# The indexer's scores from split, stacked operands instead of fp32

## The reference

```
iq = i_q.reshape(bsz, seq, IDX_HEADS, IDX_DIM)          # 16 heads of 64
ik = layernorm(i_k, idx_k_ln_g[l], idx_k_ln_b[l])       # one key of 64 for all heads
iw = i_w * (IDX_HEADS ** -0.5) * (IDX_DIM ** -0.5)
...
rel = jax.nn.relu(jnp.einsum('bthd,bsd->bths', iqb, ik))
score = jnp.einsum('bths,bth->bts', rel, iwb)
score = jnp.where(causal[None], score, -jnp.inf)
_, idx = lax.top_k(score, topk)                         # topk = 128
```

## Time and profile before

| | |
|---|---|
| median of 3 runs | 2920.77 us |
| lowest, highest | 2913.46, 2920.83 us |
| profiled execution | 2919.38 us |
| its span, first to last instruction | 2918.1 us |
| mean granted TensorE clock | 0.974 of full speed |
| busy share: TensorE, VectorE, ScalarE, GpSimd | 95%, 38%, 36%, 44% |
| chain that ended last: share of TensorE | 78% |
| the eight query projections and their scores | 1295 to 1437 us of the span |

### The profile page before, as it was taken

The page is one execution under the profiler, slowest core; times in us unless marked ns, Lnnn a source line. Parts: engine busy times, 40 slices in busy tenths (PEclk is TensorE's granted clock), DMA queues, the critical chain, the costliest instruction groups (busy, mean ns, idle before and its releaser), DMA issues.

```text
span 2918.1 us, 31494 instructions
## 1 busy us (share of the span) xinstructions
PE 2772.0 (95%) x12512; PEld 2208.8 (76%) x12512; DVE 1095.5 (38%) x1696; ACT 1045.7 (36%) x1727; POOL 1272.9 (44%) x638
## 2 busy tenths in 40 slices
PE   7579999999999999999999999999999999999999
PEld 5557788887777778866787777776777787788787
DVE  7967744442121131142376343334232213212200
ACT  5123333333333342232343444344343333433311
POOL 5664333433433354442334433343444444554743
PEclk9679999999999999999999999999999999999999
DMA  9745322222222214421222222222223322333343
GB/s 348 260 171 199 137 73 73 80 73 76 83 87 81 89 69 148 144 90 65 73 77 79 94 91 86 92 100 70 94 104 102 109 99 99 105 117 116 120 151 105
DMA packets 102961, 323.27 MB, mean 111 GB/s; under 512 B 11424, under 2 KB 14496, under 8 KB 102304
## 3 DMA queue, kind: packets, MB, share of 16 engines
q1 hardware_dynamic: 99072, 307.64, 30.8%
q10 hardware_dynamic: 3744, 13.63, 1.3%
HBM read 304.45 MB, written 16.78 MB: 110 GB/s over the span
## 4 chain that ended last, share of the span: by engine, by line
PE 78%; DVE 10%; POOL 4%; ACT 3%; DMA 2%; issue 2%; SPq 0%; DVEq 0%; ACTq 0%
PE bank L582 23%; PE bank L584 22%; PE bank L583 22%; POOL wlo L1652 2%; PE bank L824 2%; DVE TA L1295 2%; PE bank L812 2%; PE bank L743 2%; PE bank L845 1%; DVE TA L1475 1%; POOL Hlo L1673 1%; PE bank L804 1%; DMA TA<-in_strip 1%; PE bank L671 1%; DVE Y L1295 1%
## 5 line engine op out<-in xcount | busy, mean ns | idle before, releaser
L1652 POOL TENSOR_TENSOR wlo<-wraw,whi 128x1024 fp32r<-128x1024 f32 (+2 forms) x454 | 1054.9, 2325 | 1483.4 <-ACT whi L883 1483.4
L582 PE MATMUL bank<-Hhi,whi 128*128 128x512 f32 x3024 | 1245.8, 412 | 25.2 <-POOL Hlo L1673 16.7
L583 PE MATMUL bank<-Hlo,whi 128*128 128x512 f32 (+1 forms) x3152 | 1229.3, 390 | 0.0
L584 PE MATMUL bank<-Hhi,wlo 128*128 128x512 f32 x3024 | 1190.2, 394 | 0.0
L582 PEld LDWEIGHTS bank<-Hhi,whi 128*128 128x128 f32 x3024 | 574.8, 190 | 189.4 <-issue 48.8
L883 ACT ACTIVATE whi<-wraw 128x1024 fp32r<-128x1024 f32 (+2 forms) x454 | 456.8, 1007 | 702.2 <-PE bank L584 701.2
L583 PEld LDWEIGHTS bank<-Hlo,whi 128*128 128x128 f32 x3152 | 604.2, 192 | 126.1 <-issue 13.5
L584 PEld LDWEIGHTS bank<-Hhi,wlo 128*128 128x128 f32 x3024 | 573.6, 190 | 124.6
L1295 DVE SCALAR_TENSOR_TENSOR TA<-TA,par 128x1024 f32<-128x1024 f32 x60 | 128.0, 2133 | 9.1 <-DMA TA<-in_w_ada 3.4
L1248 DVE TENSOR_TENSOR TA<-bank,rows 128x512 f32<-128x512 f32 x48 | 33.0, 688 | 235.3 <-PE bank L584 235.3
L945 ACT ACTIVATE TA<-bank 128x512 f32<-128x512 f32 x64 | 38.0, 594 | 205.4 <-PE bank L584 205.4
(11 more groups left out here) (225 smaller groups left out, 2632.1 us busy)
## 6 DMA issues: line engine op xcount, KB each, us to landing
wraw<-in_w_in SPq DMA_DIRECT2D x304, 512.0 KB, 3.2
TA<-in_w_ada SPq DMA_DIRECT2D x64, 512.0 KB, 4.9
Y<-in_w_ada SPq DMA_DIRECT2D x32, 512.0 KB, 4.0
wraw<-in_w_out SPq DMA_DIRECT2D x32, 512.0 KB, 3.2
wraw<-in_w_o SPq DMA_DIRECT2D x32, 512.0 KB, 3.2
wraw<-in_w_mem ACTq DMA_DIRECT2D x16, 512.0 KB, 5.6
tmp_mgs<-TA SPq DMA_DIRECT2D x32, 256.0 KB, 2.0
TA<-tmp_mgs SPq DMA_DIRECT2D x32, 256.0 KB, 3.6
```

Source lines behind the costliest of these rows:

```text
L582: e.matmul(out, hi[:, c], xhi[k], start=first and j == 0, stop=False)
L583: e.matmul(out, hi[:, c], xlo[k], start=False, stop=False)
L584: m = e.matmul(out, lo[:, c], xhi[k], start=False, stop=last and end)
L1652: e.tensor_tensor(M.wlo[b][:, 0:w], M.wraw[b][:, 0:w], M.whi[b][:, 0:w].bitcast(F32), ALU.subtract).then_inc(S.lo)
```

## The change

Query and key are split for the scores as the large operands are. For the key, the 64 features lie twice on the 128 partitions; the rounded part goes to `ikp[0]` on all 128 and the remainder to `ikp[1]`. For each head, a buffer holds the rounded query on its own 64 partitions and its remainder on the other 64. One product on 128 rows of this stack with `ikp[0]` gives the sum of rounded x rounded and remainder x rounded; a second, on 64 rows, adds rounded x remainder of the key. The buffers are in Ohi and Olo.

The rounded parts are made by ScalarE and the remainders by VectorE, in a new post step for iq (first slot of the following projection, before the score step there) and at the end of the key's post step. The other engines get an empty step of the same place.

```diff
+        ohi, olo = self.pair["o"]
+        self.iqs, self.ikp = ((ohi[0], ohi[1]), (ohi[2], ohi[3])), (olo[0], olo[1])
...
     def index(j):
-        mark = moved("iq")
-
         def run():
-            Q, K = M.W2["Q"][j % 2], M.W2["K"][0]
-            pe.wait_ge(S.ik, 1)
-            pe.wait_ge(*mark)
+            K = M.ikp
+            pe.wait_ge(S.ikr, 1)
+            pe.wait_ge(S.iqr, 2 * j + 2)
             for hh in range(2):
-                r = slice(64 * hh, 64 * hh + 64)
+                r, Q = slice(64 * hh, 64 * hh + 64), M.iqs[j % 2][hh]
                 for i in (3, 2, 1):
-                    w = P * (i + 1)
+                    c, w = slice(i * P, (i + 1) * P), P * (i + 1)
                     bank = (BS0, BS1)[i % 2]
                     pe.wait_ge(*free[bank])
-                    e.matmul(M.banks[bank][:, 0:w], Q[r, i * P:(i + 1) * P], K[r, 0:w], start=True,
-                             stop=True).then_inc(S.ix)
+                    e.matmul(M.banks[bank][:, 0:w], Q[:, c], K[0][:, 0:w], start=True, stop=False)
+                    e.matmul(M.banks[bank][:, 0:w], Q[r, c], K[1][r, 0:w], start=False, stop=True).then_inc(S.ix)
...
# ScalarE, at the end of the key's post step
+        act.wait_ge(S.ik, 1)
+        e.activation(M.ikp[0], M.dst("ik"), ACT.Copy).then_inc(S.ikh)
+
+    def iq(j):
+        mark = moved("iq")
+
+        def run():
+            act.wait_ge(*mark)
+            act.wait_ge(S.ix, 6 * (j - 1))
+            for hh in range(2):
+                r = slice(64 * hh, 64 * hh + 64)
+                e.activation(M.iqs[j % 2][hh][r, :], M.dst("iq", j)[r, :], ACT.Copy).then_inc(S.iqh)
+            yield from rest(0)
+        return run()
...
# VectorE, at the end of the key's post step
+        dve.wait_ge(S.ik, 1)
+        dve.wait_ge(S.ikh, 1)
+        e.tensor_tensor(M.ikp[1], b, M.ikp[0].bitcast(F32), ALU.subtract).then_inc(S.ikr)
+
+    def iq(j):
+        mark = (S.evd, n["evd"])
+
+        def run():
+            dve.wait_ge(*mark)
+            for hh in range(2):
+                r, o = slice(64 * hh, 64 * hh + 64), slice(64 - 64 * hh, 128 - 64 * hh)
+                Q = M.iqs[j % 2][hh]
+                dve.wait_ge(S.iqh, 2 * j + hh + 1)
+                e.tensor_tensor(Q[o, :], M.dst("iq", j)[r, :], Q[r, :].bitcast(F32), ALU.subtract).then_inc(S.iqr)
+            yield from rest(0)
+        return run()
...
# TensorE's, ScalarE's and VectorE's posts get iq, GpSimd's and SyncE's get iq=idle(0)
```

More of the change, by code:

```diff
@@ L346, in __init__ @@
         self.ikq, self.ikl, self.ik = sem("ikq"), sem("ikl"), sem("ik")
+        self.ikh, self.ikr, self.iqh, self.iqr = sem("ikh"), sem("ikr"), sem("iqh"), sem("iqr")
         self.ix, self.ir, self.ia, self.top = sem("ix"), sem("ir"), sem("ia"), sem("top")
@@ L864, in tensor_program @@
             mem_k=mem_k, mem_v=mem_v, decay=silu, hq=silu, hv=turn("hv"), hz=silu, aq=norm("aq", ones),
-            ak=norm("ak", ones), av=turn("av"), az=silu, ik=ik, cq=norm("cq", ones), cg=silu, ckv=ckv,
+            ak=norm("ak", ones), av=turn("av"), az=silu, ik=ik, iq=lambda j: rest(0), cq=norm("cq", ones), cg=silu, ckv=ckv,
             bk=norm("bk", ones64), bv=turn("bv"), gate=silu, bq=norm("bq", ones64), bg=silu, qa=norm("qa", ones),
@@ L1169, in scalar_program @@
             mem_k=mem_k, mem_v=mem_v, decay=decay, hq=silu("hq"), hv=lambda h: rest(0), hz=silu("hz"),
-            aq=norm("aq"), ak=norm("ak"), av=lambda h: rest(0), az=silu("az"), ik=ik, cq=norm("cq"), cg=silu("cg"),
+            aq=norm("aq"), ak=norm("ak"), av=lambda h: rest(0), az=silu("az"), ik=ik, iq=iq, cq=norm("cq"), cg=silu("cg"),
             ckv=ckv, bk=norm("bk"), bv=lambda: rest(0), gate=gate, bq=norm("bq"), bg=silu("bg"), qa=norm("qa"),
@@ L1639, in vector_program @@
             mem_k=lambda h: rest(1), mem_v=lambda h: rest(1), decay=decay, hq=silu("hq"), hv=turn("hv"),
-            hz=silu("hz"), aq=norm("aq"), ak=norm("ak"), av=turn("av"), az=silu("az"), ik=ik, cq=norm("cq"),
+            hz=silu("hz"), aq=norm("aq"), ak=norm("ak"), av=turn("av"), az=silu("az"), ik=ik, iq=iq, cq=norm("cq"),
             cg=silu("cg"), ckv=ckv, bk=norm("bk"), bv=turn("bv"), gate=gate, bq=norm("bq"), bg=silu("bg"),
@@ L1761, in gpsimd_program @@
             mem_k=mem_k, mem_v=mem_v, decay=decay, hq=silu("hq"), hv=idle(0), hz=silu("hz"), aq=idle(1), ak=idle(1),
-            av=idle(0), az=silu("az"), ik=idle(1), cq=idle(1), cg=silu("cg"), ckv=ckv, bk=idle(1), bv=idle(0),
+            av=idle(0), az=silu("az"), ik=idle(1), iq=idle(0), cq=idle(1), cg=silu("cg"), ckv=ckv, bk=idle(1), bv=idle(0),
             gate=gate, bq=idle(1), bg=silu("bg"), qa=idle(1), ka=idle(1), va=idle(0), ga=silu("ga"))))
@@ L1883, in sync_program @@
             mem_k=idle(1), mem_v=idle(1), decay=idle(2), hq=idle(2), hv=idle(0), hz=idle(2), aq=idle(1), ak=idle(1),
-            av=idle(0), az=idle(2), ik=idle(1), cq=idle(1), cg=idle(2), ckv=lambda i: rest(2 * i), bk=idle(1),
+            av=idle(0), az=idle(2), ik=idle(1), iq=idle(0), cq=idle(1), cg=idle(2), ckv=lambda i: rest(2 * i), bk=idle(1),
             bv=idle(0), gate=idle(2), bq=idle(1), bg=idle(2), qa=idle(1), ka=idle(1), va=idle(0), ga=idle(2))))
```

## The result

The changed kernel takes 2949.02 us in the median of four runs (2937.33 to 2950.66), before 2920.8; the ratio is 1.0091 with a 95% interval of 1.0069 to 1.0113. It is slower: the medians lie 28.2 us apart, the ratio stands for 26.6 us. It took 30.6 us more than the profiled execution of before; 4.2 of these lie ahead of the changed stretch, whose start varies between 1283.5 and 1294.4 us over the profiled executions of this study.

The account below looks back on a forecast made before the run. TensorE, busy 95% of the span, was taken to bound the kernel. Products -7.9, wait +18.8 and clock +8.0 gave +18.9 us, so 2940 us, with a range of 2920 to 2948.

Parts of the forecast that it names:

- cheaper products: Score steps: two fp32r products replace each fp32 one, gaining 0.31 us per long and 0.19 per short step, 7.9 in all.
- TensorE's wait: Before each tile's first score product TensorE waits for VectorE's subtractions: 2.35 us per tile, 18.8 for eight.
- lower clock: Behind 5.6 of 8 TensorE waits a 3.4 us stretch at 1.2 GHz, 1.43 us each: 8.0 us, bounds 0 and 11.4.
- The price of the change of rows: Score steps: alternating 128-row and 64-row fp32r products cost as in fp32, 0.38 us; steps take 2.045 and 1.09 us.
- rival B: Score steps: changing rows costs fp32r products nothing, gain 26.9 us; 2914 us, up to 2925 with low clock; chance 0.13.
- The chain of the wait: From a tile's last projection product (P) through ScalarE, GpSimd and VectorE: TensorE ready at P + 3.59, goes on at P + 5.83.
- Rival C: VectorE's 64-partition subtractions are not held by GpSimd: wait 7.2 us in all, clock stays, 2920 us; chance 0.07.
- rival E: Score stage costlier: more than one low-clock stretch after a wait, or 64-row fp32r products dearer than fp32; 2945 to 2960; chance 0.08.
- Rival D: TensorE's wait before the scores is as forecast, but the clock stays up: 2932 us; chance 0.20.

Follow-up runs that it names:

- 128-row runs: Changed kernel with both score products on 128 rows: steps in place 2929.09 us, one slot later 2897.07, one slot later with zeros made earlier 2890.91.
- e3_gpsimd_after: Changed kernel, but GpSimd's weight remainder behind each query tile waits until VectorE's two subtractions are done: 2921.89 us, ratio 1.0011.
- e1_fill9: Changed kernel with nine extra 512-column products per query tile in front of TensorE's wait for the subtractions: 2929.11 us, ratio 1.0037.
- e9_fill6: Changed kernel with six extra products per query tile in front of TensorE's wait: 2935.75 us, ratio 1.0052.
- e2_fill3: Changed kernel with three extra products per query tile in front of TensorE's wait: 2938.29 us, ratio 1.0064.
- after: The changed kernel itself, with nothing further edited, against the kernel before: 2949.02 us, ratio 1.0091.
- e6_128_rows: Changed kernel with both products of each score on 128 rows (key's remainder padded with zeros), score steps in their place: 2929.09 us, ratio 1.0037.

## Why the prediction was right

The direction came out, and so did the three causes: cheaper products, the wait, the clock behind it. The first two terms were right to 1.3 us and the third was too small by 7, so the sum fell short by 8 us of 27.

| term of the sum | forecast | measured | from |
|---|---|---|---|
| cheaper products | -7.9 | -8.2 | 148.1 - 156.3 |
| TensorE's wait | +18.8 | +20.1 | 168.2 - 148.1 |
| lower clock | +8.0 (0 to 11.4) | +15.0 | 183.2 - 168.2 |
| sum | +18.9 | +26.9 | 183.2 - 156.3 |

**The price of the change of rows** held to hundredths: short step 1326.64 - 1325.56 = 1.08 us (forecast 1.09), and the step of fp32r products pays what the fp32 rows had shown. Taking it from the shape and not from the type was right; rival B would have needed the pitch of the 128-row runs. The rule of the Trainium skill (TensorEngine Tiling, Key Properties), that changing the tiling mode drains the engine, agrees with this trace for fp32r as well: (148.1 - 129.4) / 48 = 0.39 us for each visit to 64 rows, and nothing where both products have 128.

**The chain of the wait** came out step by step, counted from P: L586 0.74 (forecast 0.75), L1171 0.85 (0.86), GpSimd 2.26 (2.27), first copy 2.38 (2.40), first subtraction released at 3.12 (3.07), TensorE at 5.95 (5.83). The 0.12 at the end is the second subtraction: I let it overlap the first by 0.09 as in the pair of the earlier trace rows, but it starts when the first has ended and takes its whole 0.69. Rival C (64 partitions are exempt from the hold) is refuted by the first subtractions of 2.06 us and more, and e3_gpsimd_after shows what it would have been worth: the time that I gave it, 2920, against 2921.89.

**The clock** was the mis-sized term. The step said: the clock falls in the row at 323 us and not in the one at 1579, the wait is longer than the first, so 5.6 low stretches of 3.4 us. Six of eight waits had one; the 5.6 was a choice, so that it came this near is luck. But four of the six lasted 6.8 us and cost 3.0 us each, where I priced all at 1.43: 4 x 3.0 + 2 x 1.6 = 15.2. I had taken the length from one row where it was 3.4 us, though the trace of before has twice that length as well:

```profile
351.20:354.60 3.40, 3.40 (x13) 3.06 (x14) 2.83 (x5) 0.00 (x0) 1.19 (x1) 0.50 0.31 106
354.60:358.00 3.40, 3.40 (x9) 2.64 (x8) 0.00 (x0) 0.00 (x0) 0.00 (x0) 0.50 0.14 53
```

And the reading behind it was wrong: the two rows looked like the two sides of a length that decides. They are not: the 1.77 us marks no limit, since the clock fell behind 1.54 us in three tiles of seven. What came is the first half of rival E, more low clock than one stretch of 3.4 us behind a wait, to which I gave 0.08 and 2945 to 2960; the clock's 15.0 us lie above the 11.4 that I had called its bound, and the pitch went up to 20.9 us, not 19.2. Rival D (no low clock) did not come; e1_fill9, where the wait is kept and the clock stays up, took 2929.11 us against the 2932 that I gave it. The range ended at 2948, a microsecond below the median of the four runs, so of the forecast the direction and two terms held, and the likeliest value of 2940 did not.

| run | TensorE idle, tiles 1 to 7 | tiles of 1 to 7 with a low stretch |
|---|---|---|
| e3_gpsimd_after | 0.83 | 1 |
| e9_fill6 | 0.86 | 3 |
| e2_fill3 | 1.54 | 3 |
| after | 2.20 | 5 |
| e6_128_rows | 2.39 | 7 |

What decides between tiles of the same idle time stays open; the runs give counts from one profiled execution each, not a cause. These stretches begin between 0.2 us before the end of the wait and 2.4 us behind it, and no run moved a wait in time with its length kept, so whether its place in time plays a part is not shown. Nor does the table say why behind the waits of after some stretches are double and behind those of e6_128_rows, in tiles 1 to 7, none is.

## What to carry to other kernels

Price an operand's preparation by who must wait for it: here 8 us of TensorE's work were saved and 20 lost to a wait, 12 of them to a subtraction that started behind GpSimd and the rest to the chain through ScalarE and VectorE, and one slot of distance turned the same change from 0.9% slower into 0.2% faster. Keep the shape of the products constant in a stream of full-array matmuls: padding the 64-row operand with zeros to 128 rows cost no columns and was worth another 19 us, once the zeros were made ahead of GpSimd's operation. And where the engine that bounds the time stands idle again and again, count the lower clock behind it: here it came even behind idle times under a microsecond.

## What the hardware showed that I had not expected

- The granted clock fell behind idle times of TensorE of only 0.83 and 0.86 us (4 of 14 tiles), and stayed at its upper level behind some of 2.20.
- A low stretch costs in two sizes: 1.6 us where it lasts 3.4, 3.0 us where it lasts 6.8. In the changed kernel they made 15 of 27 us.
- Nine extra products per tile, 72 in all, whose results nobody reads, made the stage 15.0 us shorter than in the change without them, by keeping TensorE at work through a wait that did not get shorter.
